# One kernel for two transformer models: weight sums on VectorE, GpSimd's tables in pairs, output matrices in three pieces

## What is computed

```python
# first model, each of 2 layers; D_MODEL 1024, D_FF 2816
h = rms_norm(x, ffn_norm[l])
gate, up = jnp.split(h @ w_gate_up[l], 2, axis=-1)
x = x + ((jax.nn.silu(gate) * up) @ w_down[l]).astype(x.dtype)

# second model, before its first product
mod = jax.nn.silu(c) @ ada_w[l] + ada_b[l]          # 6 vectors of 1024
hn = rmsnorm(h, mix_pre_g[l]) * (1.0 + sc1[:, None, :]) + sh1[:, None, :]

# its S5 part: a diagonal linear recurrence of 64 complex states in 32 groups
ab_re = mag * jnp.cos(li * dt)
ab_im = mag * jnp.sin(li * dt)
f_re = ((ab_re - 1.0) * lr + ab_im * li) / den
_, _, xr, xi = lax.associative_scan(combine, (a_re, a_im, bu_re, bu_im), axis=1)
y = (jnp.einsum('btgp,ghp->btgh', xr, c_re) - jnp.einsum('btgp,ghp->btgh', xi, c_im) + d * uf)
```

## Time and profile before

| what | value |
|---|---|
| time, median of 3 (lowest, highest) | 1849.14 us (1847.36, 1854.38) |
| the profiled execution's own time | 1850.51 us |
| its span, first to last instruction | 1848.3 us |
| TensorE busy | 1786.6 us |
| VectorE, ScalarE, GpSimd busy | 867.3, 260.5, 290.6 us |
| mean granted TensorE clock | 0.991 |
| layer 0: first block's start, blocks 1 to 10, down slots | 171, 183.5 to 312.6, to 379 us |
| layer 1: blocks 1 to 10, down slots | 551 to 687, to 753.5 us |

### The profile page before, as it was taken

One profiled execution on the slowest core, in us unless ns is written; L12 is line 12 of the kernel. 1 busy time (PEld: TensorE's weight loads), 2 busy tenths in 40 slices (PEclk: granted clock), 3 DMA queues, 4 the chain that ended last, 5 costly groups with the idle time before them and its releaser, 6 DMA issues.

```text
span 1848.3 us, 24992 instructions
## 1 busy us (share of the span) xinstructions
PE 1786.6 (97%) x9054; PEld 918.4 (50%) x9055; DVE 867.3 (47%) x1675; ACT 260.5 (14%) x549; POOL 290.6 (16%) x423
## 2 busy tenths in 40 slices
PE   9999999999999899899999999999999999999997
PEld 4466998444669894555433333333333333333332
DVE  4554989865548886696522212221212212221222
ACT  1421111014111110232101001010001000010101
POOL 0201343002008888532000000000000000000000
PEclk9999999999999899999999999999999999999999
DMA  8143887641424345225999999999999699999995
GB/s 326 69 178 160 324 335 274 240 182 69 182 112 183 137 172 190 94 92 234 371 423 429 427 429 428 429 427 429 428 429 428 251 425 428 429 427 429 427 429 236
DMA packets 41749, 559.67 MB, mean 303 GB/s; under 512 B 4902, under 2 KB 5798, under 8 KB 7116
## 3 DMA queue, kind: packets, MB, share of 16 engines
q1 hardware_dynamic: 40956, 557.53, 73.1%
q10 hardware_dynamic: 720, 1.18, 0.2%
HBM read 557.62 MB, written 1.07 MB: 302 GB/s over the span
## 4 chain that ended last, share of the span: by engine, by line
PE 61%; DMA 22%; DVE 13%; issue 2%; ACT 1%; DVEq 0%; SPq 0%; ACTq 0%; POOLq 0%
DMA mega<-in_exp_w 17%; PE PS L2430 12%; PE PS L2065 12%; PE PS L2470 8%; PE PS L1776 7%; PE PS L2102 7%; DMA tenth<-in_exp_w 5%; PE PS L1953 3%; PE PS L2416 2%; PE PS L2314 2%; DVE mega L1448 1%; PE PS L2423 1%; PE PS L2046 1%; PE PS L1747 1%; DVE K L1676 1%
## 5 line engine op out<-in xcount | busy, mean ns | idle before, releaser
L2430 PE MATMUL PS<-mega,tb 128*64 128x512 f32 x1728 | 378.2, 593 | 8.9 <-POOLq L2615 8.0
L1674 DVE TENSOR_SCALAR tmp<-PS 128x512 f32<-128x512 f32 x34 | 23.5, 692 | 549.1 <-PE PS L2430 549.1
L2430 PEld LDWEIGHTS PS<-mega,tb 128*64 128x64 f32 x1728 | 123.5, 137 | 258.2 <-issue 238.8
L2470 PE MATMUL PS<-mega,tb 128*64 128x512 f32 x896 | 198.4, 595 | 0.0
L2065 PE MATMUL PS<-mega 128*128 128x128 f32 x1440 | 169.0, 279 | 10.4 <-DVE hT L1334 10.4
L2065 PEld LDWEIGHTS PS<-mega 128*128 128x128 f32 x1440 | 167.0, 196 | 10.8 <-issue 10.7
L1776 PE MATMUL PS<-mega,hT 128*128 128x512 f32 (+2 forms) x416 | 171.1, 551 | 0.2 <-ACT hT L542 0.2
L2470 PEld LDWEIGHTS PS<-mega,tb 128*64 128x64 f32 x896 | 61.9, 137 | 133.1 <-issue 127.7
L1776 PEld LDWEIGHTS PS<-mega,hT 128*128 128x128 f32 x416 | 74.6, 190 | 59.3 <-issue 47.1
L2102 PE MATMUL PS<-mega 128*128 128x512 f32 x188 | 83.6, 592 | 0.0
L852 ACT ACTIVATE K<-tmp 128x512 f32<-128x512 f32 x34 | 21.4, 630 | 430.7 <-DVE tmp L1674 430.7
(11 more groups left out here) (542 smaller groups left out, 2264.6 us busy)
## 6 DMA issues: line engine op xcount, KB each, us to landing
mega<-in_exp_w SPq DMA_DIRECT2D x154, 2048.0 KB, 26.2
mega<-in_w_gate_up SPq DMA_DIRECT2D x22, 2048.0 KB, 7.9
tenth<-in_exp_w SPq DMA_DIRECT2D x19, 2048.0 KB, 29.3
late<-in_exp_w SPq DMA_DIRECT2D x19, 2048.0 KB, 28.2
mega<-in_ada_w SPq DMA_DIRECT2D x12, 2048.0 KB, 8.3
mega<-in_w_down SPq DMA_DIRECT2D x10, 2048.0 KB, 7.2
mega<-in_w_in_part SPq DMA_DIRECT2D x9, 2048.0 KB, 8.8
mega<-in_w_out SPq DMA_DIRECT2D x6, 2048.0 KB, 8.5
```

The source lines that it names most:

```text
L2430: ins = pe.matmul(PS[64 * h:64 * h + 64, b, :], xg[:, o:o + 64], slot_of(r, s)[:, w:w + 512], start=False, stop=k == KC - 1, skip_group_ch ...
L2470: ins = pe.matmul(PS[64 * h:64 * h + 64, 2, :], aT[:, P * (c % 4) + 64 * (c // 4):P * (c % 4) + 64 * (c // 4) + 64], slot_of(r, s)[:, o:o ...
```

## The change

- In layer 0, GpSimd's loop over the sums is deleted, and next_sums no longer skips sums 1 and 2. VectorE makes all four, with the wait for FIFTH before sum 1. CHUNKS moves some chunks between blocks 1 to 9; 34 stay in blocks 1 to 10.
- table(q) becomes tables(a), for two tables at a time: the same instructions half as often, each over twice the columns (up to 1024). Both pairs come before g_row, whose second half (1024 columns) gives s_gd. g_row serves as scratch until then.
- output_matrices is cut into three parts of three instructions, after down slots 0, 1 and 2 of layer 1. decay_rows(0), which needs them, follows on ScalarE after slot 3 instead of slot 1.
- Blocks 8 and 9 of layer 1 write their activations elsewhere (into proj and K), so VectorE's wait for s_gd goes. GpSimd's memset of sct[1] gets a wait for down slot 4.
- ScalarE scales the first four of eight column groups of t = 0 before it squares x[:, 1], and TensorE takes one product of w_in_2 (two matmuls' records) earlier.

```diff
@@ -148,7 +148,7 @@
-CHUNKS = (0, 4, 3, 4, 4, 3, 4, 3, 4, 3, 2, 3, 3, 3, 3, 2, 0)
+CHUNKS = (0, 3, 3, 4, 4, 4, 3, 4, 3, 4, 2, 3, 3, 3, 3, 2, 0)
...
@@ -314,7 +314,7 @@
-                 [tenth[:, 2048 + 512 * i:2560 + 512 * i] for i in range(4)] + [tenth[:, 512 * i:512 * i + 512] for i in range(2)] + [bm_rows[:, 1024:1536]]]
+                 [tenth[:, 2048 + 512 * i:2560 + 512 * i] for i in range(4)] + [pf[:, 5924:6436], K[:, K_DEC + 1024:K_DEC + 1536]] + [bm_rows[:, 1024:1536]]]
...
+        pair_tab = [ring[:, 3 + 2 * a, :].rearrange("p (b i j t) -> p b i j t", b=2, i=2, j=4) for a in range(2)]
...
@@ -695,9 +695,9 @@
                 for j in range(DN_SLOTS - 2):
                     freed_down(j)
-                    if l == DEPTH - 1 and j == 1:
-                        act.wait_ge(g.dve2, DVE2["u_cm"] + 1)
-                        decay_rows(0)
+                if l == DEPTH - 1:
+                    act.wait_ge(g.dve2, DVE2["u_cm"] + 1)
+                    decay_rows(0)
...
@@ -711,8 +711,6 @@
-            act.wait_ge(g.dve2, DVE2["x_add_1"] + 1)
-            link.to(nc.scalar.activation(xn[:, 1, :], x[:, 1, :], ACT.Square, accum_out=st[:, 231:232]), g.act2, ACT2["n_sq1"] + 1)
...
                 if c == 3:
                     link.to(shifted(c, 0, 4, 0), g.act2, ACT2["n_ha"] + 1)
+                    act.wait_ge(g.dve2, DVE2["x_add_1"] + 1)
+                    link.to(nc.scalar.activation(xn[:, 1, :], x[:, 1, :], ACT.Square, accum_out=st[:, 231:232]), g.act2, ACT2["n_sq1"] + 1)
...
             def beside(i):
                 if i == 2:
                     state_matrices()
-                if i == 4:
-                    output_matrices()
...
@@ -1271,10 +1272,6 @@
                 def next_sums(i, which):
-                    if l == 0 and which[0] < 3:
-                        which = which[2:]
-                    if not which:
-                        return
...
@@ -1327,8 +1324,7 @@
                     condition(i, 1, 2)
-                    if l == DEPTH - 1:
-                        v.wait_ge(g.p_p, 7 * n + FIFTH)
+                    v.wait_ge(g.p_p, 7 * n + FIFTH)
                     next_sums(i, (1,))
...
-                    if l == DEPTH - 1 and i == 8:
-                        v.wait_ge(g.s_gd, 1)
...
@@ -1369,6 +1363,8 @@
                     condition(FF_BLOCKS + j, 2, 3)
+                    if l == DEPTH - 1 and j < 3:
+                        output_matrices(j)
...
-                v.wait_ge(g.u_e, q + 1)
+                v.wait_ge(g.u_e, q // 2 + 1)
...
@@ -2189,10 +2185,10 @@
             pe.wait_ge(g.act2, ACT2["n_ha"] + 1)
-            rows(("win2", 2), 0, 4, (0,))
+            rows(("win2", 2), 0, 4, (0, 1))
...
@@ -2517,46 +2513,31 @@
-                if l == 0:
-                    pool.wait_ge(g.s_wo, TT)
-                    for u in range(1, FF_BLOCKS + 1):
...
-                        link.to(pool.tensor_tensor(s1, b12, b11, ALU.subtract), g.t_w, m + 1)
-                        link.to(pool.tensor_tensor(s2, b22, s1, ALU.subtract), g.t_w, m + 2)
...
-                    cw = pw[:, 0].broadcast_to([P, 4, w])
-                    sw = pw[:, 2].broadcast_to([P, 4, w])
-                    a0, b0, a1, b1 = er[:, :, 0:w], ei[:, :, 0:w], er[:, :, w:2 * w], ei[:, :, w:2 * w]
-                    aux = paux[:, 0:4 * w].rearrange("p (j t) -> p j t", j=4)
+                    cw, sw = (pw[:, i].unsqueeze(3).broadcast_to([P, 2, 4, w]) for i in (0, 2))
+                    a0, b0, a1, b1 = er[:, :, :, 0:w], ei[:, :, :, 0:w], er[:, :, :, w:2 * w], ei[:, :, :, w:2 * w]
+                    aux = g_row[:, 0:8 * w].rearrange("p (b j t) -> p b j t", b=2, j=4)
...
             pool.wait_ge(freed[3], LOADS_BEFORE[3] + 1)
-            table(0)
+            pool.wait_ge(g.s_wo, TT * DEPTH)
+            tables(0)
+            pool.wait_ge(freed[5], LOADS_BEFORE[5] + 2)
+            tables(1)
             pool.wait_ge(g.r_row, 64)
...
-            table(1)
-            pool.wait_ge(freed[5], LOADS_BEFORE[5] + 2)
-            table(2)
-            table(3)
             link(pool.memset(sct[0], 0.0))
+            pool.wait_ge(g.p_v, slot_done(1, DN_SLOTS - 2))
             link.to(pool.memset(sct[1], 0.0), g.u_pa, 1)
```

More of the change, by code:

```diff
@@ L372, in program @@
         vv2 = tmp[:, 0:1024].rearrange("p (t c) -> p t c", t=TT)
-        s5v, ph = blf[:, 300:492], blf[:, 500:516]
+        s5v, ph = blf[:, 300:492], blf[:, 500:532]
         mc = st[:, 120:152]
         c_in, c_junk, c_row = tmp[:, 512:1536], tenth[:, 0:1024], tenth[:, 1024:2048]
-        paux = par[:, 0:512]
         og, sgate = xn[:, :, 0:512], xn[:, :, 512:1024]
@@ L970, in state_matrices, with output_matrices @@
                 link(v.tensor_scalar(s5v[:, GLB][:, 0:4], p2[:, Q_GLB:Q_GLB + 4], 0.5, None, ALU.mult))
-            def output_matrices():
+            def output_matrices(part):
                 v.wait_ge(g.r_ssm, 32)
@@ L977, in output_matrices @@
                 t3 = cneg.rearrange("p (j m) -> p j m", j=16)
[L978 to L986, removed]
+                if part == 0:
+                    link(v.tensor_tensor(t1, cre, fr, ALU.mult))
+                    link(v.tensor_tensor(t2, cim, fi, ALU.mult))
+                    link(v.tensor_tensor(t1, t1, t2, ALU.subtract))
+                if part == 1:
+                    link(v.tensor_tensor(t3, cre, fi, ALU.mult))
+                    link(v.tensor_tensor(t2, cim, fr, ALU.mult))
+                    link(v.scalar_tensor_tensor(t3, t3, -1.0, t2, ALU.mult, ALU.subtract))
+                if part == 2:
+                    link(v.tensor_copy(cre, t1))
+                    link.to(v.tensor_scalar(cim, t1, -1.0, None, ALU.mult), g.dve2, DVE2["u_cm"] + 1)
+                    link(v.tensor_scalar(p2[:, Q_GG:Q_GG + 1], p2[:, Q_GG:Q_GG + 1], 0.5, None, ALU.mult))
             def beside(i):
@@ L2191, in _ @@
             pe.wait_ge(g.act2, ACT2["n_ha"] + 1)
-            rows(("win2", 2), 0, 4, (0,))
+            rows(("win2", 2), 0, 4, (0, 1))
             pe.wait_ge(g.dve2, DVE2["n_xn_1"] + 1)
             turn_rows(1, 6, g.pe2)
-            rows(("win2", 2), 0, 4, (1,))
+            rows(("win2", 2), 0, 4, (2,))
             pe.wait_ge(g.act2, ACT2["n_hb"] + 1)
@@ L2203, in _ @@
             ins.then_inc(g.u_p, 1)
-            rows(("win2", 2), 0, 4, (2,))
+            rows(("win2", 2), 0, 4, (3,))
             pe.wait_ge(g.r_ssm, 32)
@@ L2217, in _ @@
             ins.then_inc(g.pe2, 1)
-            rows(("win2", 2), 0, 4, (3, 4))
+            rows(("win2", 2), 0, 4, (4,))
             pe.wait_ge(g.act2, ACT2["al_e"] + 1)
@@ L2536, in _, with tables @@
             pool.wait_ge(g.s_ha2, TT * DEPTH)
-            def table(q):
-                er, ei = (etab[q][:, i, :].rearrange("p (j t) -> p j t", j=4) for i in range(2))
-                cos, sin = (s5v[:, c][:, 4 * q:4 * q + 4].unsqueeze(2) for c in (COS_, SIN_))
-                link(pool.memset(er[:, :, 0:1], 1.0))
-                link(pool.memset(ei[:, :, 0:1], 0.0))
-                link(pool.tensor_copy(er[:, :, 1:2], cos))
-                link(pool.tensor_copy(ei[:, :, 1:2], sin))
+            def tables(a):
+                er, ei = (pair_tab[a][:, :, i] for i in range(2))
+                cos, sin = (s5v[:, c][:, 8 * a:8 * a + 8].rearrange("p (b j) -> p b j", b=2) for c in (COS_, SIN_))
+                link(pool.memset(er[:, :, :, 0], 1.0))
+                link(pool.memset(ei[:, :, :, 0], 0.0))
+                link(pool.tensor_copy(er[:, :, :, 1], cos))
+                link(pool.tensor_copy(ei[:, :, :, 1], sin))
+                pw = ph.rearrange("p (i b j) -> p i b j", i=4, b=2)
                 w = 2
                 while w < T:
-                    c1, s1 = (m[:, :, w - 1:w] for m in (er, ei))
-                    pw = ph.rearrange("p (i j) -> p i j", i=4).unsqueeze(3)
+                    c1, s1 = (m[:, :, :, w - 1] for m in (er, ei))
                     link(pool.tensor_tensor(pw[:, 0], c1, cos, ALU.mult))
```

12 lines of the change are left out of this document (2 added, 10 removed).

## The result

The changed kernel takes 1859.85 us (median of 15 runs, 1856.04 to 1862.22) against 1850.32 us for the kernel before (15 runs, 1844.95 to 1854.38): a ratio of 1.0052, 95% interval 1.0043 to 1.0060. It is 9.5 us slower; the forecast was 3 us faster, 1846, with 1858 as its upper end. The profiled execution took 1859.64 us.

A forecast was written before the change was run, and what follows sets the result against it. TensorE, busy 1786.6 of 1848.3 us, bounds the kernel, so only its waits count. Terms 11.0 + 0 - 11.1 + 0.5 - 3.6 = -3.2 us take the profiled 1850.5 to 1847.3, less 1.4: 1846 us, range 1836 to 1858.

The forecast's parts named there:

- Part 1: First layer's ten fast blocks: four weight sums on VectorE make it the bound, costing 11 us (+9.5 to +13).
- VectorE carries the sums: Faster rival, first layer: VectorE's block takes 13.1 us, so the layer costs 4 us instead of 11; 1839; chance 0.14.
- half clock adds up: Slower rival, first layer: each of ten waits costs 1 us beyond VectorE's chain, +10, 1856; chance 0.05.
- Part 2: Second layer's blocks: output matrices leave, so the stall at 612 us and its half clock go, -11.1 us; moved instructions hidden.
- the stall only moves: Slower rival: if pairs take 80 us, late g_row delays loads and half the output-matrix gain goes; 1852; chance 0.05.
- Part 4: Entry to the second model: reordered ScalarE work and absent GpSimd give -2.3 us, perhaps 2.7 more from the clock; -3.6 taken.
- Part 3: GpSimd tables in pairs: twelve 1024-column instructions within the second layer's blocks are nearly hidden, +0.5 us.
- I take 0.9 each, since they meet the same instructions of the same blocks, and +0.5 us: Second layer's blocks: each 1024-column GpSimd instruction costs VectorE 0.9 us, hidden below 1.3; +0.5 for chance meetings.
- GpSimd's long instructions hold VectorE: Slower rival, second layer's blocks: each long instruction costs VectorE 2.0 to 2.4 us, giving 1857 to 1862; chance 0.10.
- the 8.4 of "32 us": Second layer's blocks: VectorE's slack of 8.4 us over the 32 us of the 512- and 1024-column table steps.
- 686 "on the old axis": GpSimd: two table pairs of 67 us each end near 686 on the kernel before's time axis, g_row near 692.

The follow-up runs named there:

- old_entry: Changed kernel with ScalarE's square of x[:, 1] back ahead of the scaled columns and the w_in_2 product at its old place: 1861.3 us, ratio 1.0059 to before.
- no_wide_step: Changed kernel without the last doubling of both table pairs (twelve 1024-column and twelve small GpSimd instructions left out, so it computes less): 1849.1 us.
- single_tables: Changed kernel with four single tables again and g_row behind the first: 1853.0 us, ratio 1.0016 to the kernel before.
- wide_in_halves: Changed kernel with each 1024-column GpSimd instruction of the table pairs made as two of 512 columns: 1856.0 us, ratio 1.0043 to before.
- sums_alone: Kernel before with only the first layer's four sums on VectorE and the new CHUNKS: 1863.6 us, ratio 1.0058 to before.
- wide_step_late: Changed kernel with layer-0 sums 1, 2 on GpSimd, halved last doublings, g_row between pairs, second pair's last doubling waiting for down slot 3: 1843.2 us.
- matrices_and_entry: Kernel before with only the output matrices in three pieces in the down slots and the new entry order: 1840.6 us, ratio 0.9956.
- sums_on_gpsimd: Changed kernel with sums 1 and 2 of the first layer on GpSimd again and CHUNKS as before: 1848.5 us, ratio 0.9994 to before.
- pairs_grow_between: Changed kernel with first-layer sums 1 and 2 on GpSimd, halved last doublings of the table pairs and g_row between the pairs: 1842.0 us, ratio 0.9959.

## Why the prediction was wrong

- **Part 1: right.** +11 was forecast and 11.3 measured, by the stage (129.1 to 140.4) and by undoing it. The down products were expected at 323.4 and began at 323.38. There were 15 waits (0.2 to 2.0 us each), and the clock stayed at 1.00, as assumed. VectorE began block 1 at 190.36, for 190.61 forecast. One thing was missed: only ten of the waits are for line 1330 (1334 before), the one named; five, 5.2 of the 11.6 us, are for sum 4, line 1272. The rivals "VectorE carries the sums" and "half clock adds up" fall.
- **Part 2: right.** The 8.44 us stall and its half clock are gone. Alone, part 2 gives 10 us (8.7 by the ratio), of the 11.1 forecast, and the nine instructions are hidden. The rival "the stall only moves" falls: the pairs took 71 and 67 us, not 80, and in the down slots TensorE waited for VectorE's lines 1285 and 1266 alone.
- **Part 4: the size right, in part by luck.** 4.1 us for 3.6. The working had it that the reordering takes what GpSimd's absence saves and that the rest comes from row_rsqrt, line 1419 and the clock; old_entry agrees. But 3.6 was the middle between two outcomes, 2.3 and 5.0. The clock stayed up, the better one, and the second turns came only 1.6 us sooner behind the first (7.1 us instead of 8.7), for 2.3 forecast.
- **Part 3: wrong**, and with it the sum. The step that failed is "I take 0.9 each, since they meet the same instructions of the same blocks, and +0.5 us". In the blocks it was 1.48 us each, above the 1.3 from which the rival "GpSimd's long instructions hold VectorE" was to decide; the cost was 4.6 us instead of 0.5 (3.6 and 3.3 come back in no_wide_step and single_tables). The 0.9 was a mean per GpSimd instruction from layer 0, where the two sums of a block stand largely beside line 913 and others with a PSUM input, which are not held: line 913 took 1.22 to 1.23 us beside them, as alone. In layer 1 there are no chunks, and each of the six finds an instruction with both inputs in SBUF. The row that showed the right price was in the prediction, line 980 with 2.72 for 0.69; I gave it to the rival, at 0.10. The slack was taken too large as well. Line 1330 ends at 607.67 us, and two blocks later, behind both wide steps, at 638.30: 30.63 us, 12.2 more than 2 x 9.19. Two blocks have 6.6 us of slack, not the 8.4 of "32 us"; with the 2.8 that is 9.4, and 12.2 - 9.4 = 2.8 is the wait, 2.72 measured. With that slack, and 3 us for the 512-column step, the limit was 1.1 us each, not 1.3.
- **The down slots were left out of the sum**, by a mix of two time axes. The tables were to end at 686 "on the old axis", and this was held against down products at 687. But that 687 is on the new axis (part 1 adds 11 us, part 2 takes them), where the tables' end is 697: by the prediction's own numbers the second pair's last doubling runs into slot 0. (The 686 is itself 1 us short: 553.9 and twice 66.7 are 687.3.) I priced it "within TensorE's blocks" only. Its wide instructions ran from 689.2 to 703.8 and g_row to 708.8, beside the end of block 10, the four sums of activations and the two instructions behind them. Together they cost 5.9 to 6.4 us (the stage +5.9, single_tables -6.2, no_wide_step -6.4), the larger half of the error. No run parts the two: both of those versions move g_row out of the down slots as well. That g_row by itself holds VectorE there is seen in wide_in_halves: lines 1285 and 1286 took 2.45 us each beside it, ahead of the wait of 5.07 us.

Sum of stages up to the experts: +11.3 + 0.4 - 6.5 + 5.9 - 4.1 + 0.3 = +7.3 us, less 0.5 for an earlier start of block 1; the forecast was -3.2. The part 3 terms, 4.6 instead of 0.5 and 5.9 instead of nothing, close the gap of 10.0. The other 2.7 us stand in the experts (919.8 to 922.5), which I had taken as rigid. This stage was 918.9 to 922.5 in the profiles, without an order that one part explains: sums_alone has 919.4, single_tables 922.3. Of the 2.7 us, 1.8 are busy time of TensorE (901.9 and 903.7 us) at a granted clock of 1.00 in both. What sets it is open.

The rival's price came from rows 7. The Trainium skill's rule (SBUF — State Buffer, "SBUF: two separate sides"), named beside it, is an exclusive lock for the whole instruction. The rows agree for VectorE instructions with both inputs in SBUF: line 1285, 2.00 us, ends 0.27 us behind the GpSimd instruction of 1.96 us beside it.

## What to carry to other kernels

Before you lengthen instructions on GpSimd, or set them in a row, list the VectorE instructions that they will meet: each with both inputs in SBUF lasted here until just behind the end of the GpSimd instruction beside it, however short it is alone, so a mean taken from a stretch with few meetings doesn't carry over. Follow such a row to its end on the time axis of the changed kernel, and ask at each stage that it reaches which wait of TensorE hangs on VectorE there. And cost each part of a combined change by itself: two parts together cost some 17 to 18 us here and hid a third, worth 9 to 10, that needed neither.

## What the runs showed of the hardware

- A 256-column VectorE instruction of 0.42 us with both inputs in SBUF took 2.00 to 2.46 us in a row of 1024-column GpSimd instructions and 1.14 to 1.38 in a row of 512-column ones; one that began shortly before the end of such an instruction lost less (line 1337 before: 0.52 to 0.74). The same with one input in PSUM took 0.42 in the middle of a GpSimd instruction.
- GpSimd pays too: a 1024-column instruction took 1.90 to 3.22 us in this turn-taking, and a 512-column one 1.04 alone (wide_step_late) and up to 2.24 beside VectorE (wide_in_halves).
- An instruction with a single SBUF input was slowed as well: line 1419's 1024 columns took 1.64 us beside 512-column GpSimd instructions and 0.75 without GpSimd.
- The first layer's blocks with sums on GpSimd took 129.1 us in four traces and 131.3 or 132.0 in two, from the same code up to there; with all sums on VectorE they took 140.3 or 140.4 in all seven. The first kind has its waits of TensorE, one to three, at the same places: 2.0 us at 207, 2.4 at 247 to 249, 0.7 at 275. What differs is which of them come, and the clock: behind the same 2.0 us, 64 records took 9.01 us in three traces (before, matrices_and_entry, wide_step_late), which have no later wait, and 7.38 in two (sums_on_gpsimd, pairs_grow_between), which have the one of 2.4. Why the clock fell in some executions and not in others is open.
